# A two-block transformer kernel on one core: the first mixer's products in another order, its modulation cut into quarters, and the last step of the filter moved among the experts

## The reference, cut to what matters

```
mod = silu(c) @ w_ada[l] + b_ada[l]                    # six vectors for each layer: "modulation"
u = rms_norm(h) * (1 + scale) + shift
# conv_mixers, layer 0 ("mixer ab")
gate_out, gate_in, val, glu_a, glu_g = split(u @ w_in_ab)      # 5 x 512 columns
y_a = gate_out * conv3(gate_in * val)
z   = conv31(glu_a * sigmoid(glu_g)) + conv_b_bias
y_b = silu(layer_norm(z))
h  += mod[2] * (concat(y_a, y_b) @ w_out_ab)
# then 16 experts (gate, up, down, each 1024 x 1024), 32 tokens each
# layer 1: attention and a long convolution whose filter is
hid = sin(fr * (sin(fr * (z @ w1 + b1)) @ w2 + b2));  filt = (hid @ w3) * decay;  hf = rfft(filt)
# then 16 experts again; the second block has dense ffns, attention and gates
```

## Time and profile before

| | us |
|---|---|
| median of 3 runs | 3008.6 (3008.09 to 3009.92) |
| the profiled execution, device time | 3010.56 |
| its span in the profile | 3009.2 |
| TensorE busy | 2739.6 (91%) |
| VectorE busy | 739.7 (25%) |
| ScalarE busy | 428.9 (14%) |

### The profile page before, as it was taken

One profiled execution on the slowest core, in us unless ns is written; L12 is line 12 of the kernel. 1 busy time (PEld: TensorE's weight loads), 2 busy tenths in 40 slices (PEclk: granted clock), 3 DMA queues, 4 the chain that ended last, 5 costly groups with the idle time before them and its releaser, 6 DMA issues. The chain is left out here.

```text
span 3009.2 us, 27371 instructions
## 1 busy us (share of the span) xinstructions
PE 2739.6 (91%) x12052; PEld 1783.8 (59%) x12052; DVE 739.7 (25%) x1298; ACT 428.9 (14%) x792; POOL 31.9 (1%) x17
## 2 busy tenths in 40 slices
PE   7998798898878779878879999999999999999999
PEld 3333533333247553322327888778888888778888
DVE  1772312112044530110102103431101111541110
ACT  2101300000031310000001001550000000370100
POOL 0000000000000010000000100000000100000000
PEclk9998799999999889999999999999999999999999
DMA  8744399999942128999999443214444543323430
GB/s 344 284 152 194 126 418 421 421 421 421 421 184 98 42 95 368 421 421 422 421 421 328 158 151 131 96 70 168 154 154 152 170 154 140 112 84 133 147 140 15
DMA packets 113618, 690.07 MB, mean 229 GB/s; under 512 B 27988, under 2 KB 29396, under 8 KB 30812
## 3 DMA queue, kind: packets, MB, share of 16 engines
q1 hardware_dynamic: 111008, 682.67, 58.0%
q0 software_dynamic: 848, 2.90, 0.3%
q10 hardware_dynamic: 1644, 2.76, 0.3%
HBM read 687.22 MB, written 1.06 MB: 229 GB/s over the span
## 5 line engine op out<-in xcount | busy, mean ns | idle before, releaser
L533 PE MATMUL bank<-normed,ring 128*128 128x256 f32 (+1 forms) x4640 | 1107.2, 400 | 3.7 <-ACT normed L1149 2.6
L533 PEld LDWEIGHTS bank<-normed,ring 128*128 128x128 f32 x4640 | 882.5, 191 | 226.2 <-issue 108.1
L533 PE MATMUL bank<-ring,normed 128*64 128x512 f32 (+2 forms) x2368 | 533.9, 567 | 60.2 <-DMA ring<-in_stream 54.3
L533 PEld LDWEIGHTS bank<-ring,normed 128*64 128x64 f32 (+1 forms) x2368 | 195.0, 145 | 391.9 <-issue 228.8
L533 PE MATMUL bank<-ffn_hidden,ring 128*128 128x256 f32 x1408 | 304.5, 379 | 0.0
L533 PEld LDWEIGHTS bank<-ffn_hidden,ring 128*128 128x128 f32 x1408 | 267.5, 190 | 36.4
L533 PE MATMUL bank<-ring,moe_turned 128*64 128x512 f32 x1024 | 230.5, 597 | 32.2 <-DVE moe_turned L1627 25.1
L533 PEld LDWEIGHTS bank<-ring,moe_turned 128*64 128x64 f32 x1024 | 69.1, 136 | 173.1 <-issue 108.5
L1625 DVE TENSOR_TENSOR moe_hidden<-bank,moe_silu 128x512 f32<-128x512 f32 x32 | 22.1, 692 | 495.2 <-PE bank L533 495.2
L1270 ACT COPY moe_hot_w<-bank 32x512 f32<-32x512 f32 x48 | 27.6, 575 | 561.0 <-PE bank L533 560.6
L1358 ACT ACTIVATE gates<-gates 128x512 f32<-128x512 f32 x44 | 27.7, 629 | 521.2 <-DVE gates L1788 521.2
(11 more groups left out here) (251 smaller groups left out, 1646.0 us busy)
## 6 DMA issues: line engine op xcount, KB each, us to landing
ring<-in_stream SPq DMA_DIRECT2D x644, 1024.0 KB, 19.2
na_bias<-in_na_rpb SPq DMA_DIRECT2D x32, 128.0 KB, 5.9
sw_bias<-distance_bias POOLq DMA_DIRECT2D x2, 1024.0 KB, 7.4
hidden<-in_x_t SPq DMA_DIRECT2D x1, 1024.0 KB, 5.7
hidden<-in_ctx_t SPq DMA_DIRECT2D x1, 1024.0 KB, 8.5
out<-hidden SPq DMA_DIRECT2D x4, 256.0 KB, 2.1
ab_y<-in_early ACTq DMA_DIRECT2D x1, 512.0 KB
dft<-in_early ACTq DMA_DIRECT2D x1, 512.0 KB
```

Of the source, the lines that this page charges most:

```text
L533: return nc.tensor.matmul(o, lhsT, rhs, start=start, stop=stop, skip_group_check=True)
```

## The change

The first mixer is written out in eight steps of two products each, and a chunk holds the two products of one step: glu_g and glu_a of one block ("glu"), or gate_in and val ("conv"), in the order of `AB_STEPS`. Behind each of the first four steps stands one quarter of modulation, behind each of the last four stand two. The four gate_out products come last: the sum for the layer norm's mean stands ahead of them, the sums of squares behind the first, and two quarters of the pair (1, 1) behind the second and the fourth. The output product takes y_b ahead of y_a. Filter steps 0 and 1 stand behind the first two steps, the two taps behind the fourth and fifth. The transform (`filter_freq`) moves behind the down products of experts 0 and 1 of the second group of four experts in layer 0; the taps live where `idft` was, and `idft` is loaded at the start of the second mixer on ScalarE's queue. The number of chunks is unchanged, and no product is added or removed.

```diff
@@ -221,13 +224,15 @@
                     add(("expert", l, e, which, q), w[l, e, 2 * P * q:2 * P * (q + 1), :])
 
     ada(0, 0)
+    column = lambda g, j: a["w_in_ab"][0][:, AW * AB_COLUMN[g] + P * j:AW * AB_COLUMN[g] + P * j + P]
+    for n, (kind, j) in enumerate(AB_STEPS):
+        add(("in_ab", kind, j), np.concatenate([column(g, j) for g in AB_GROUPS[kind]], axis=1))
+        for l, pair, q in AB_QUARTERS[n]:
+            ada_quarter(l, pair, q)
     for jp in range(JB // 2):
-        for g in AB_GROUPS:
-            c0 = AW * AB_COLUMN[g] + 256 * jp
-            add(("in_ab", g, jp), a["w_in_ab"][0][:, c0:c0 + 256])
-        for pair in ((0, 1), (0, 2)) if jp == 0 else ((1, 0),):
-            ada(*pair)
-    ada(1, 1)
+        add(("in_ab", "out", jp), np.concatenate([column("gate_out", 2 * jp + jj) for jj in range(2)], axis=1))
+        for q in (2 * jp, 2 * jp + 1):
+            ada_quarter(1, 1, q)
     for c in range(KB // 2):
         add(("out_ab", c), a["w_out_ab"][0][:, 256 * c:256 * c + 256])
     ada(1, 2)
...
 
-AB_GROUPS = ("gate_in", "val", "glu_g", "glu_a", "gate_out")
+
+AB_GROUPS = {"glu": ("glu_g", "glu_a"), "conv": ("gate_in", "val")}
+AB_STEPS = (("glu", 0), ("glu", 1), ("conv", 0), ("glu", 2), ("conv", 1), ("glu", 3), ("conv", 2), ("conv", 3))
+_QUARTERS = [(l, pair, q) for l, pair in ((0, 1), (0, 2), (1, 0)) for q in range(KB // 2)]
+AB_QUARTERS = [_QUARTERS[n:n + 1] for n in range(4)] + [_QUARTERS[n:n + 2] for n in range(4, 12, 2)]
+
+AB_PAIRS = {3: (0, 1), 5: (0, 2), 7: (1, 0)}
 AB_COLUMN = {"gate_out": 0, "gate_in": 1, "val": 2, "glu_a": 3, "glu_g": 4}
 
...
@@ -544,6 +566,8 @@
     def ada_part(l, pair, q):
 
         pe.wait_ge(*A.at("cond"))
+        if q == 0 and (l, pair) != (0, 0):
+            pe.wait_ge(*A.at(("ada_row",) + ((l, pair - 1) if pair else (l - 1, 2))))
...
-        elif n == 2:
-            pe.wait_ge(*A.at(("sine", 1)))
-            pe.wait_ge(*A.at(("ada_row", 0, 2)))
-            for t in range(TT):
-                mm(bank[5 + t][:, :], ab.hid[0:64, t * P:t * P + P], ab.fw3[0:64, :], True, True).then_inc(*done.up(("filter", 2, t)))
+        else:
+            t = n - 2
+            if t:
+                pe.wait_ge(*V.at(("filter_taps", t - 1)))
+            else:
+                pe.wait_ge(*A.at(("sine", 1)))
+            mm(bank[5][:, :], ab.hid[0:64, t * P:t * P + P], ab.fw3[0:64, :], True, True).then_inc(*done.up(("filter", 2, t)))
+
+    def filter_freq(f):
+        b = 5 + f % 2
+        if f >= 2:
+            pe.wait_ge(*A.at(("filter_freq", f - 2)))
         else:
             pe.wait_ge(*V.at(("filter_taps", TT - 1)))
-            for f in range(4):
-                b = 5 + f % 2
-                if f >= 2:
-                    pe.wait_ge(*A.at(("filter_freq", f - 2)))
-                for t in range(TT):
-                    ins = mm(bank[b][:, :], M.dft[:, t, f * P:f * P + P], ab.htok[:, t, :], t == 0, t == TT - 1)
-                ins.then_inc(*done.up(("filter", 3, f)))
-
-    def project_back(tag, kind, rhs, w):
+        for t in range(TT):
+            ins = mm(bank[b][:, :], M.dft[:, t, f * P:f * P + P], M.htok[:, t, :], t == 0, t == TT - 1)
+        ins.then_inc(*done.up(("filter", 3, f)))
+
...
                 if n >= 4:
                     pe.wait_ge(*V.at((tag, "back", n - 4)))
-                for k in range(KB):
-                    ins = mm(bank[b][:, 0:w], tile[:, k, P * half:P * half + P], rhs[:, k, :], k == 0, k == KB - 1)
+                for i, k in enumerate(order):
+                    if tag == "ab" and n == 0:
+                        pe.wait_ge(*(A.at(("y_b", k - JB)) if k >= JB else V.at(("y_a", k))))
+                    ins = mm(bank[b][:, 0:w], tile[:, k, P * half:P * half + P], rhs[:, k, :], i == 0, i == KB - 1)
                 ins.then_inc(*(ring.free(name) if half else done.up((tag, "back", n))))
+            if (tag, c) == ("ab", 0):
+                ada_turn(1, 1)
...
+        def product(b, tile, half):
+            for k in range(KB):
+                pe.wait_ge(*A.at(("ab", "normed", k, NS - 1)))
+                ins = mm(both(bank[b][:, :]), tile[:, k, P * half:P * half + P], U[:, :, k, :], k == 0, k == KB - 1)
+            return ins
+
+        for n, (kind, j) in enumerate(AB_STEPS):
+            name = ("in_ab", kind, j)
+            tile = ring.tile(name)
+            pe.wait_ge(*ring.landed(name))
+            b0, b1 = (2, 3) if kind == "glu" else (0, 1)
+            if j:
+                pe.wait_ge(*(A.at(("sigmoid", j - 1)) if kind == "glu" else A.at(("gate_in", j - 1))))
+            product(b0, tile, 0).then_inc(*done.up(("in_ab", kind, j)))
+            if j:
+                pe.wait_ge(*(V.at(("pad_b", j - 1)) if kind == "glu" else V.at(("pad_a", j - 1))))
+            product(b1, tile, 1).then_inc(*ring.free(name))
+            if n in (0, 1):
+                filter_step(n)
+            elif n in (3, 4):
+                filter_step(n - 1)
+            if n - 1 in AB_PAIRS:
+                ada_turn(*AB_PAIRS[n - 1])
+            for quarter in AB_QUARTERS[n]:
+                ada_part(*quarter)
...
+            name = ("in_ab", "out", j // 2)
+            pe.wait_ge(*ring.landed(name))
+            pe.wait_ge(*(V.at(("pad_b", JB - 1)) if j >= 2 else V.at(("pad_a", JB - 1))))
+            product(j, ring.tile(name), j % 2).then_inc(*(ring.free(name) if j % 2 else done.up(("in_ab", "out", j))))
+            if j == 0:
+                ada_turn(*AB_PAIRS[len(AB_STEPS) - 1])
+                pe.wait_ge(*V.at(("filter_taps", TT - 1)))
+                for i in range(JB):
+                    pe.wait_ge(*A.at(("ln_square", i)))
+                    mm(bank[5][:, :], ones, ab.sq[:, i % 2, :], i == 0, i == JB - 1).then_inc(*done.up(("ln_sum", i)))
+            if j % 2:
+                ada_part(1, 1, j - 1)
+                ada_part(1, 1, j)
+        pe.wait_ge(*A.at("ln_root"))
+        pe.wait_ge(*V.at(("centred", 0)))
+        project_back("ab", "out_ab", ab.Y, 512, (*range(JB, KB), *range(JB)))
...
+                if (l, g) == (0, 1) and e < 2:
+                    filter_freq(2 * e)
+                    filter_freq(2 * e + 1)
...
-            pe.wait_ge(*I["middle"].at("all"))
+            pe.wait_ge(*I["idft"].at("all"))
...
-        load("middle", M.SIN, a["middle"][:, T:2 * T])
-        load("middle", flat(M.idft), a["middle"][:, 2 * T:], "all")
+        load("middle", M.SIN, a["middle"][:, T:2 * T], "all")
...
+        for n, (kind, j) in enumerate(AB_STEPS):
+            act.wait_ge(*TE.at(("in_ab", kind, j)))
+            if kind == "glu":
+                if j:
+                    act.wait_ge(*V.at(("pad_b", j - 1)))
+                nc.scalar.activation(ab.SG, bank[2][:, :], ACT.Sigmoid).then_inc(*done.up(("sigmoid", j)))
+                if j < 2:
+                    sine(j)
+            else:
+                if j:
+                    act.wait_ge(*V.at(("pad_a", j - 1)))
+                nc.scalar.copy(ab.GI, bank[0][:, :]).then_inc(*done.up(("gate_in", j)))
+            if n - 1 in AB_PAIRS:
+                ada_turned(*AB_PAIRS[n - 1])
+            if n in AB_PAIRS:
+                ada_row(*AB_PAIRS[n])
...
+        load("idft", flat(M.idft), a["middle"][:, 2 * T:], "all")
...
-        elif n == 2:
+        else:
+            t = n - 2
             dve.wait_ge(*I["filter"].at("all"))
-            for t in range(TT):
-                dve.wait_ge(*TE.at(("filter", 2, t)))
-                v.tensor_tensor(ab.htok[:, t, :], bank[5 + t][:, :], ab.decay[:, t, :], ALU.mult).then_inc(*done.up(("filter_taps", t)))
+            dve.wait_ge(*TE.at(("filter", 2, t)))
+            v.tensor_tensor(M.htok[:, t, :], bank[5][:, :], ab.decay[:, t, :], ALU.mult).then_inc(*done.up(("filter_taps", t)))
 
     def back(tag, kind, l, streams):
...
+            if kind == "glu":
+                dve.wait_ge(*A.at(("sigmoid", j)))
+                v.tensor_tensor(ab.PB[:, :, 15:T + 15], both(bank[3][:, :]), both(ab.SG), ALU.mult).then_inc(*done.up(("pad_b", j)))
+                if n in (0, 1):
+                    filter_step(n)
+                elif n == 3:
+                    filter_step(2)
+                dve.wait_ge(*done.at(("pad_b", j)))
+                z_j = both(ab.Z[:, j, :])
+                v.tensor_scalar(z_j, ab.PB[:, :, 0:T], tap("conv_b", 0, j), vec("conv_b_bias", j), ALU.mult, ALU.add).then_inc(*done.up())
+                for k in range(1, TAPS_B):
+                    dve.wait_ge(*done.now())
+                    ins = v.scalar_tensor_tensor(out=z_j, in0=ab.PB[:, :, k:k + T], scalar=tap("conv_b", k, j), in1=z_j, op0=ALU.mult, op1=ALU.add)
+                    ins.then_inc(*done.up(("z", j) if k == TAPS_B - 1 else None))
+            else:
+                dve.wait_ge(*A.at(("gate_in", j)))
+                v.tensor_tensor(ab.PA[:, :, 1:T + 1], both(bank[1][:, :]), both(ab.GI), ALU.mult).then_inc(*done.up(("pad_a", j)))
+                if n == 4:
+                    filter_step(3)
```

(46 more changed lines are left out.)

80 lines of the change are left out of this document (30 added, 50 removed).

## The result

The changed kernel takes 2989.8 us (median of 4 runs, 2987.9 to 2990.8) against 3009.3 for the kernel before (4 runs): a ratio of 0.9934, interval 0.9917 to 0.9952. Beside the first experiments it ran once more, 2989.1 (5 runs) against 3010.9 on that chip, 0.9926 (0.9913 to 0.9940).

A forecast was written before the change was run, and what follows sets the result against it. TensorE was taken to pace the first mixer, full DMA engines the layer 0 experts, whose end shifts with their start. 34.6 us removed and 11.3 added gave -23.3, so a 2985 us median, range 2976 to 2995.

The forecast's parts named there:

- What goes: First mixer, TensorE: transform with its copy wait 7.7 us, other waits 16.9, slow clock behind them 10.0; 34.6 us saved.
- What is added: First filter step in the mixer: TensorE waits 9.4 us for `in_filter`, then a clock ramp of 1.9; 11.3 us added.
- My reading of `cos`: Load behind the filter's six: bytes end at about 62.2 us, landed at 63.75, 1.6 later; so `in_filter` at 62.0.
- The bound of 73.1 for the landing: Latest filter landing, from the old place of `hf_z`'s product at 73.07: at most 20.5 us of wait, 22.4 with ramp.
- rival 2: Filter loads land later, up to 73.1, sharing engines with the stream: gain 12 to 20 us, 2989 to 2996; chance 0.12.
- `cos` as the near bound: Filter landing no later than `cos` at 63.75, being ahead in one queue; 13.0 us added with the ramp.
- VectorE, nearly as late: Mixer: VectorE's third `ab_pad_a` ends 111.5 us after the filter's landing, TensorE asks at 114; 2 us of room.
- The sum: Whole program: -34.6 + 11.3 = -23.3 us; profiled execution 3010.56 to 2987.3, median 2.0 below it, so 2985.
- rival 1: The author's own forecast, `in_filter` landing between 59 and 65 us: gain 20 to 27, 2982 to 2989; chance 0.65.
- rival 4: Slower: quarters of modulation drop TensorE's clock at their ten places, 3030 us if each does; chance 0.04.
- rival 5: The saving doesn't arrive, expert stage pinned by something begun before it: 3005 to 3011 us; chance 0.05.
- The signs given for the profile: 9 us wait before `hf_z`, output product ending near 284, last z near 173, sums 3.5 each, experts' stream waits some 16.

The follow-up runs named there:

- e3_transform_back: Changed kernel with the filter's transform put back into the first mixer, on TensorE behind the last gate_out product; 2995.4 us.
- e5_norm_open: Changed kernel with all gate_out products and the last pair's quarters first, then the layer norm's mean and squares' sums and the output product at once; 3002.6 us.
- e4: Changed kernel with modulation quarters joined into whole pairs behind the fourth, sixth and eighth steps, none between; 2990.1 us, 0.9935 of the kernel before.
- e6: Changed kernel with whole modulation pairs and the filter steps placed later (behind steps two, four, five, seven); 2983.3 us, 0.9914 of the kernel before.
- e1_later: Changed kernel with the four filter steps placed later, behind the second, fourth, fifth and seventh mixer steps; 2978.4 us, 0.9893 of the kernel before.

## Why the prediction was right, point by point

**What goes.** Of the 34.6 us on my list, e3_transform_back gives 6.3 for the transform (listed 7.7), and e5_norm_open 12.5 for the norm's cover (listed 2.17 + 4.51 and the ramps of the squares and the output product, 11.4). Together that is 18.8 of the 32.9 us that went (22.9 and the 10.0 that were added). What is left, the wait for the last z, the wait for the stream, those for the row copies and their ramps, was not undone singly, so what each is worth rests on the timeline, which shows all of these waits gone: without the wait for the filter's loads TensorE's idle time in the mixer fell from 17.6 us to 0.1, as listed. The slow clock is another matter, see the sum.

**What is added.** The mechanism was right: TensorE waits for `in_filter` with nothing to cover it, and a ramp of 2.1 us for 1.9 follows. The landing was forecast for 62.0 and came at 61.85 and 61.0, but 61.85 is a hit by luck. Counted from the mixer's first product I had 25.1 us; the five profiles in which TensorE waited for `dft` have 24.1 to 24.4, and the 61.85 came out of a mixer that began 0.8 us later. My reading of `cos` was off: by the 0.05 MB per us of the earlier trace rows its last byte comes at about 62.8 us and not at 62.2 (the queue had moved 1.44 MB by 62.5 and 1.49 by 63), so its landing is 1.0 us behind it and not 1.6. In the changed kernel 1.34 MB are through at 61.0, and the landing is 0.85 later. TensorE was late as well: its two first products took 16.3 and 16.8 us where I had 15.8. So the wait was 7.9 and 7.3 us and not 9.4. The bound of 73.1 for the landing, and with it the cause of rival 2, fell; `cos` as the near bound held. Had only the 73.1 held, the sum would have been 22.4 - 11.3 = 11 us worse, not 9.

**VectorE, nearly as late.** 112.6 us for my 111.5, and a room of 2.5 us for my 2. How near that was, e4 and e6 show.

**The sum.** The mixer is shorter by 22.9 us, for 23.3. That it is so near is partly luck, since two errors cancel. With 10.0 us added and not 11.3 the list gives 24.6, so 1.7 us less went than I had listed. They are all in TensorE's busy time, in pieces that I had put at full clock or at the pace of a long row: the two first products (16.28 us where 32 records take 13.8 undisturbed), the single quarters (1.85 us from start to start, for 1.77), the taps and the two sums. Of the 22.9, 22.0 are left at the first expert product (373.22 to 351.19, the later start again) and 21.0 in the spans (3009.2 to 2988.2); the expert stage was 1 us longer. Over the nine profiles that stage ran 458.0 to 459.4 us with no order in it that follows the edits, so I count both as scatter between executions. From there to the forecast of 2985 against 2989.8 two steps were off, by about 2.3 us each: the profiled executions differ by 21.0 and not 23.3, and the 2.0 us by which the kernel before lay under its profiled execution did not come again (2989.5 profiled, 2989.8 the median).

**The rivals.** By its time, 2989.8, the result stands just inside rival 2's 2989 to 2996; by its cause, a landing between 59 and 65, it is rival 1. No quarter slowed the clock: each single one is 1.92 or 1.93 us, apart from the one behind the wait (rival 4). The saving arrived (rival 5). The signs given for the profile came in the main: the wait ahead of `hf_z`, the end of the mixer at 285.6 for 284, the last z at 173.6 for 173, sums of 3.7 and 3.8 for 3.5. The waits for the stream were 19.0 us where I had 16: they gave back 4 to 5 us of the transform's 7, and the stage did not grow beyond its scatter.

## What to carry to other kernels

When a step is moved forward in a hand-written order, look at what its semaphore covers: a small product here waited 7.9 us for a megabyte that it never reads, and either two later places in the list or a second semaphore gave back 9 to 11 us on top of the change (2978.4 us, the best of these kernels). Ahead of a stage that the DMA engines fill, nearly everything saved reached the end (21.0 of 22.9 us), and matmuls moved into such a stage cost nothing visible where its waits for the stream (23.6 us) were longer than the matmuls (7.0). Independent products kept for last are the cover of a reduction chain, 12.5 us here. Cutting other filler fine paid only where the slower engine's results were nearly due.

## What the runs showed of the hardware that I had not expected

A wait of 3.4 us for VectorE cost nearly as much again: the product of 7.03 us behind it took 10.15, at a granted clock of 0.70 (e6_later_pairs). The waits of 2.2 and 5.8 us in e5_norm_open cost 1.6 and 1.8 behind them, that of 7.9 us in the changed kernel 2.1, and that of 1.5 us in e4_whole_pairs only 0.1. The cost does not follow the length of the wait; what else decides it is not shown.

The first product of the mixer started anywhere from 35.6 to 37.8 us, although the instructions ahead of it are the same in all these runs. The last quarter ahead of it, in the changed kernel and in e1_later:

```profile
29.62 3.64 PE L555 MATMUL bank<-ring,small 128*32 128x512 f32 x16 [3.05 <-DMA ring<-in_stream]
```

```profile
29.74 1.92 PE L556 MATMUL bank<-ring,small 128*32 128x512 f32 x16 [3.06 <-DMA ring<-in_stream]
```

Behind the same wait of 3.05 us the same work took 3.64 us or 1.92. The granted clock from 29.6 to 38.0 us was 0.50 in the two runs whose mixer began at 37.7 and 37.8, and 0.80 and 0.81 in those that began at 35.6 and 35.8. So the scatter of the start is that of TensorE's clock; why it fell in some executions and not in others stays open.
